# The expert loop's turns move from TensorE to VectorE in 32x32 squares, with a new order of the contraction and loops of four tiles

## The chip, the core and the metric

One core of one Trainium2 chip runs the kernel. The metric is the device time of one execution in microseconds (us), the median of several runs. Five engines work side by side, each with its own instruction stream: TensorE (PE, with its weight loads shown apart as PEld), VectorE (DVE), ScalarE (ACT), GpSimd (POOL) and SyncE (SP). SP issues most of the transfers and POOL issues the indirect ones. They wait for each other only through semaphores.

## The reference, cut to what matters

One layer of a hybrid backbone over 512 latent tokens of width 1024 (and 256 context tokens): a mixer (attention and a linear recurrence), then a mixture of experts. The change is almost all in the mixture:

```python
aff = sigmoid(h @ router_w)                    # h = rms(x) * norm_ffn * (1 + sc) + sh, (512, 1024)
# two experts for each token, out of 16, gates normalised
for e in range(16):
    y = (silu(h @ w1[e]) * (h @ w3[e])) @ w2[e]   # w1, w3: (1024, 512)   w2: (512, 1024)
    out = out + gates[:, e:e+1] * y
x = x + g_fx * out
```

All data are float32.

## The kernel before, in words

**Stages.** Up to about 387 us the kernel does the mixer, the residual and the router's products. VectorE then works out a plan: each expert's tokens are cut into tiles of 32 tokens, at least two tiles for each expert. This input gives 44 tiles, by expert in the order of the loop 3, 2, 2, 2, 4, 3, 2, 3, 5, 3, 2, 2, 4, 3, 2, 2. From about 412 us on the expert loop runs over these tiles; I number them 0 to 43. At the end SP copies the sums out.

**A tile.** A token's row of 1024 numbers lies in DRAM as four quarters of 256, and in SBUF a tile is 128 partitions (4 quarters x 32 tokens) x 256. For each tile:

- POOL gathers the 128 quarter rows from `xn_quarters` into one of two buffers `xg` (`gather`, L482), once the index column `cur_g` has been written by ACT (`gather_index`, L738) and the buffer has been emptied.
- ACT copies `xg` to `xrow` (`next_rows`, L731), which empties `xg`. PE turns it with two 128x128 transposes into PSUM (`turn_rows`, L1628), VectorE scales and shifts it by `ab2` (`rows_ready`, L1259) into `hsT`.
- PE multiplies by w1 and w3 (`products`, L1614: 32 matmuls, each recorded twice, so x64), ACT applies silu (`gate_half`, L723), VectorE multiplies the halves (`gated`, L1266).
- PE turns the result with one transpose (`turn_act`, L1634), ACT copies it to `eT` (`turned`, L727), PE multiplies by w2 (`rows_out`, L1638: 16 matmuls, x32).
- VectorE scales the rows by the gate into one of two buffers `ysb` (`scaled`, L1270) and POOL adds them to `out_quarters` in DRAM by an indirect transfer with addition (`scatter`, L486), with an index column `cur_s` that ACT wrote (`scatter_index`, L744).

On PE the order of a tile is `products(n)`, `turn_rows(n+1)`, `rows_out` for tile n-1, `turn_act(n)`. On POOL a scatter and a gather alternate: `fetch_rows` (L503), then `store_rows` (L509). Both indirect transfers go through POOL's queue, q0; the weights go through SP's, q1.

**Weights.** SP streams them in 48 chunks of 2 MB, three for each expert: chunk 3e and 3e+1 are the two halves of the contraction of w1 and w3, chunk 3e+2 is w2 (`fetch`, L309). There are 11 homes for them (`homes`, L245), so the first 11 chunks come early, and from chunk 11 on a chunk waits until the chunk 11 places before it has been used (L340 to L345). In DRAM a chunk is read as `(k p) n`: a run of consecutive bytes is one row, 2 KB for w1 and w3 and 4 KB for w2.

Of the kernel before, what the change touches and what calls it, by code (L numbers as in the profile page):

```python
# [56 lines left out]
def build(nc, x, c, ctx_in, c_ctx, w_mod, b_mod, norm_mix, norm_ffn, w_in, w_out, q_gain, k_gain, na_bias,  # L57
# [3 lines left out]
    xn_dram = nc.dram_tensor("xn_quarters", (TRASH + 2 * P, QD), F32, kind="Internal").ap()  # L61
    acc_dram = nc.dram_tensor("out_quarters", (TRASH + 2 * P, QD), F32, kind="Internal").ap()
# [6 lines left out]
    with ctx:  # L69
# [57 lines left out]
        row_sum = small[:, 32:34]  # L127
        hsum = sb("hsum", [P, 2, 2, H])
# [8 lines left out]
        xrow = hx[:, 4864:5120]  # L137
# [5 lines left out]
        ysb = [pre[:, 21632:21888], pre[:, 21888:22144]]  # L143
# [21 lines left out]
        cur_s = [nc.alloc_sbuf_tensor_at(f"cur_s{par}", [P, 1], I32, offset=hx_at + 4 * (4096 + 192 + 8 * par))  # L165
                 for par in range(2)]
# [15 lines left out]
            rank_m oh_ready oh_used rank_ps plan_in xn_out tok_ready t_ps sil_ready act_ready t2_ps  # L182
            t2_ev fin_out misc_in rw_in h_ps xm_ready hs_ready yt_ps y_ev cur_g_ready cur_s_ready
            acc_in gf_ps gf_ev lane_set sil_warm pad_ready xr_ready bank_z row_sum_ready scale_ready
            hc_ready h2_ev2""".split()
# [7 lines left out]
         xn_out, tok_ready, t_ps, sil_ready, act_ready, t2_ps, t2_ev, fin_out, misc_in, rw_in, h_ps,  # L193
         xm_ready, hs_ready, yt_ps, y_ev, cur_g_ready, cur_s_ready, acc_in, gf_ps, gf_ev, lane_set,
         sil_warm, pad_ready, xr_ready, bank_z, row_sum_ready, scale_ready, hc_ready, h2_ev2) = [sem(n) for n in names]
        xg_in = [sem(f"rows_in{par}") for par in range(2)]
        y_in = [sem(f"sums_in{par}") for par in range(2)]
# [56 lines left out]
        def chunk13(e, part):  # L254
            return homes[(3 * e + part) % NH].rearrange("p (k w n) -> p k w n", k=4, w=2)
# [4 lines left out]
        H_, X_, T_, Y_ = B[2], B[0], B[4], B[5]  # L260
# [21 lines left out]
        def _(sp):  # L282
# [49 lines left out]
            sp.wait_ge(xn_out1, 8 * NT + 16)  # L332
            sp.wait_ge(h2_ps, 2 * NT)
            fetch(8)
            sp.wait_ge(acc_in, 16 * NT + 32)
# [10 lines left out]
            half = sp.value_load(plan[0:1, 3 * NE - 1:3 * NE], min_val=NE - 2, max_val=MAXT // 2 - 2)  # L346
            added = sp.snap(16 * half + 32)
            for par in range(2):
                sp.wait_ge(y_in[par], added)
# [7 lines left out]
        def _(pool):  # L357
# [49 lines left out]
            g.dma_start(rw[:], router_w.rearrange("(k p) e -> p k e", p=P)).then_inc(rw_in, 16)  # L407
# [60 lines left out]
            for z in range(2):  # L468
                g.dma_start(xn_dram[TRASH + P * z:TRASH + P * (z + 1), :], xn[:, 0, 0:QD]).then_inc(
                    (xn_out, xn_out1)[z], 16)  # L470
# [4 lines left out]
            for z in range(2):  # L475
                g.dma_start(acc_dram[TRASH + P * z:TRASH + P * (z + 1), :], x2[:, 0, 0:QD]).then_inc(acc_in, 16)
            link(g.iota(pad_i[:], [[0, 32], [P, 2]], base=TRASH, channel_multiplier=1))
# [14 lines left out]
            pool.wait_ge(xn_out1, 8 * NT + 16)  # L492
            pool.wait_ge(acc_in, 16 * NT + 32)
# [3 lines left out]
            for n in (2, 3):  # L497
                pool.wait_ge(xr_ready, n - 1)
                gather(slot_tok[:, n:n + 1], n % 2)
            pool.wait_ge(plan_in, 1)  # L500
            half = pool.value_load(plan[0:1, 3 * NE - 1:3 * NE], min_val=NE - 2, max_val=MAXT // 2 - 2)

            def fetch_rows(h, par):  # L503
                indexed = pool.snap(2 * h + par - 3)
                pool.wait_ge(cur_g_ready, indexed)
                pool.sem_inc(pool_step, 1)
                gather(cur_g[par][:], par)

            def store_rows(h, par):  # L509
                indexed, scaled, stored = (pool.snap(n) for n in (2 * h + par + 1, 2 * h + par + 2, 16 * h))  # L510
# [3 lines left out]
                pool.wait_ge(y_in[par], stored)  # L514
                pool.sem_inc(pool_step, 1)
                scatter(par)

            for u in range(2):
                pool.wait_ge(cur_g_ready, u + 1)
                gather(cur_g[u][:], u)  # L520
                pool.wait_ge(cur_s_ready, u + 1)
                pool.wait_ge(y_ev, u + 2)
                scatter(u)
            with pool.Fori(1, half) as h:
                for par in range(2):
                    fetch_rows(h + 2, par)
                    store_rows(h, par)
            fetch_rows(half + 2, 0)
            for n in range(4):
                store_rows(half + n // 2, n % 2)  # L530

        @block.scalar
        def _(act):
# [193 lines left out]
            def turned(n):  # L727
                act.wait_ge(t2_ps, n + 1)
                a.activation(eT, T_[:, 0:P], ACT.Copy).then_inc(t2_ev, 1)  # L729

            def next_rows(h, par):  # L731

                act.wait_ge(xg_in[par], 16 * h + 16)
                if not isinstance(h, int) or h + par:
                    act.wait_ge(t_ps, 2 * h + par)
                a.activation(xrow, xg[par], ACT.Copy).then_inc(xr_ready, 1)  # L736

            def gather_index(h, par):  # L738

                act.wait_ge(xg_in[par], 16 * h)  # L740
                act.wait_ge(xr_ready, 2 * h + par - 1)
                a.activation(cur_g[par][:], slot_tok[:, bass.ds(2 * h + par, 1)], ACT.Copy).then_inc(cur_g_ready, 1)

            def scatter_index(h, par):  # L744

                if not isinstance(h, int) or h:
                    act.wait_ge(y_in[par], 16 * h)
                a.activation(cur_s[par][:], slot_tok[:, bass.ds(2 * h + par, 1)], ACT.Copy).then_inc(cur_s_ready, 1)  # L748
# [3 lines left out]
            next_rows(0, 0)  # L752
            act.wait_ge(plan_in, 1)
            half = act.value_load(plan[0:1, 3 * NE - 1:3 * NE], min_val=NE - 2, max_val=MAXT // 2 - 2)
            next_rows(0, 1)

            def activation(gt):
# [3 lines left out]
                if not isinstance(gt, int) or gt:  # L761
                    act.wait_ge(yt_ps, gt)
                turned(gt)

            activation(0)
            next_rows(1, 0)
            gather_index(2, 0)
            activation(1)
            next_rows(1, 1)
            gather_index(2, 1)  # L770
            scatter_index(0, 0)
            activation(2)
# [921 lines left out]
```

## Time and profile before

| what | us |
|---|---|
| median of 3 runs | 710.21 (709.7 to 711.41) |
| the profiled execution, whole | 711.65 |
| its span, first to last instruction | 709.9 |
| PE busy | 635.1 (89%) |
| DVE busy | 345.1 (49%) |
| ACT busy | 229.4 (32%) |
| POOL busy | 176.4 (25%) |

A busy share is an average over stages. The queries used below are: the chain of work that ended last, in order of time (start, us, what); the timeline of one engine or of a stretch (start, us, engine, line, operation, output<-input, and in brackets the idle time before it); groups of instructions by line; and the DMA view of a short stretch. PEclk is the TensorE clock that was granted, in tenths of full speed.

### The profile page before, as it was taken

To read this page: it belongs to the slowest core of one execution; us is meant where nothing else is said; L and a number is where in the kernel's file an instruction comes from. 1 tells how busy PE (TensorE), PEld (TensorE's weight loads), DVE (VectorE), ACT (ScalarE), POOL (GpSimd) and SP (SyncE) were. 2 spreads that over 40 slices of the span, in tenths; PEclk is the share of its full clock that TensorE was granted. 3 is DMA by queue.
4 is the path that set the end of the run, shared out by engine and by line. 5 is a ranking of instruction groups with operands and counts; after the bars stand their busy time and mean duration, and the time that the engine had idled before them with its cause. 6 is when DMAs were issued, how large, how long until landed. Compare 5 with 4: busy or idle time off the path is not lost.

```text
span 709.9 us, 15144 instructions
## 1 busy us (share of the span) xinstructions
PE 635.1 (89%) x5905; PEld 350.0 (49%) x5905; DVE 345.1 (49%) x823; ACT 229.4 (32%) x587; POOL 176.4 (25%) x201
## 2 busy tenths in 40 slices
PE   0799999899998999999999249999999999999991
PEld 0446544455444445555558225555555555555550
DVE  4513999556678957877755712222222222222220
ACT  5312201258887114555654001221112211222110
POOL 3033682000000001000003022344444444344431
PEclk9999999989999999999996559999999999999996
DMA  7999338711105359400059963999999999999924
GB/s 218 387 317 296 127 118 294 239 60 42 76 1 178 116 188 269 123 2 1 1 167 408 414 256 93 371 382 381 379 378 379 378 382 376 379 382 383 330 37 133
DMA packets 83507, 167.55 MB, mean 236 GB/s; under 512 B 4148, under 2 KB 26320, under 8 KB 83456
## 3 DMA queue, kind: packets, MB, share of 16 engines
q1 hardware_dynamic: 71856, 145.78, 56.6%
q0 software_dynamic: 11472, 21.00, 11.8%
q8 instruction: 38, 0.62, 0.4%
q14 instruction: 13, 0.11, 0.0%
q10 hardware_dynamic: 128, 0.04, 0.0%
HBM read 155.52 MB, written 12.60 MB: 237 GB/s over the span
## 4 chain that ended last, share of the span: by engine, by line
PE 67%; DVE 17%; DMA 5%; issue 5%; ACT 4%; SPq 1%; POOLq 0%; DVEq 0%; ACTq 0%
PE bank L1623 23%; PE bank L1646 12%; PE bank L1432 7%; PE bank L1540 6%; DMA ring<-in_w_mod_dram 4%; DVE acct L886 3%; PE bank L1357 3%; DVE gax L886 3%; PE bank L1631 2%; PE bank L1517 2%; PE bank L1492 2%; PE bank L1503 2%; DVE pre L904 2%; PE bank L1636 2%; PE bank L1321 1%
## 5 line engine op out<-in xcount | busy, mean ns | idle before, releaser
L1432 PE MATMUL bank<-ring,hx 128*128 128x512 f32 x256 | 114.9, 605 | 2.7 <-DVE mix L939 2.7
L487 POOL DMA_INDIRECT out_quarters<-pre,cur_s x44 | 69.6, 1582 | 146.3 <-ACT cur_s L748 124.2
L1268 DVE TENSOR_TENSOR pre<-pre,bank 128x128 f32<-128x128 f32 x44 | 12.7, 288 | 161.8 <-ACT pre L725 161.8
L1432 PEld LDWEIGHTS bank<-ring,hx 128*128 128x128 f32 x256 | 49.0, 194 | 60.2 <-issue 59.5
L1623 PE MATMUL bank<-pre 128*32 128x256 f32 x1248 | 75.1, 387 | 2.1 <-DVE pre L1264 1.4
L1623 PE MATMUL bank<-ring,pre 128*32 128x256 f32 x1152 | 68.5, 384 | 0.3
L1540 PE MATMUL bank<-ring,mix 128*128 128x512 f32 x128 | 60.7, 594 | 0.0
L1623 PEld LDWEIGHTS bank<-pre 128*32 128x32 f32 x1248 | 41.7, 111 | 26.8 <-issue 3.0
L725 ACT ACTIVATE pre<-bank 128x128 f32<-128x128 f32 x44 | 12.2, 278 | 118.4 <-PE bank L1623 118.4
L1623 PEld LDWEIGHTS bank<-ring,pre 128*32 128x32 f32 x1152 | 38.1, 111 | 23.1 <-issue 2.7
L1357 PE MATMUL bank<-hx,ring 128*128 128x256 f32 (+1 forms) x128 | 43.7, 502 | 1.4 <-DVE hx L864 1.4
L729 ACT ACTIVATE pre<-bank 128x128 f32<-128x128 f32 x44 | 12.2, 278 | 97.3 <-PE bank L1636 97.3
L1646 PE MATMUL bank<-pre 128*32 128x256 f32 x704 | 42.5, 382 | 0.6 <-DVE pre L1275 0.6
L1275 DVE SCALAR_TENSOR_TENSOR pre<-bank,hx,pre 128x256 f32<-128x256 f32 x44 | 21.3, 484 | 44.3 <-PE bank L1646 44.3
L456 POOL DMA_DIRECT2D pre<-pre x1 | 0.6, 561 | 153.6 <-ACT pre L661 153.6
L1357 PEld LDWEIGHTS bank<-hx,ring 128*128 128x128 f32 x128 | 24.7, 195 | 20.1 <-issue 17.4
L1646 PE MATMUL bank<-ring,pre 128*32 128x256 f32 x544 | 32.9, 382 | 0.0
L886 DVE SCALAR_TENSOR_TENSOR acct<-ring,cs,acct 128x256 f32<-128x256 f32 x56 | 29.4, 525 | 2.0
L466 POOL DMA_DIRECT2D xn_quarters<-pre x4 | 2.2, 544 | 110.5 <-DVE pre L1063 110.5
L1540 PEld LDWEIGHTS bank<-ring,mix 128*128 128x128 f32 x128 | 21.7, 190 | 14.7 <-issue 14.7
L1646 PEld LDWEIGHTS bank<-pre 128*32 128x32 f32 x704 | 20.8, 109 | 15.5 <-issue 3.5
L1631 PE MATMUL bank<-ident,hx 128*128 128x128 f32 x90 | 19.9, 304 | 8.9 <-ACT hx L736 8.9
(282 smaller groups left out, 1033.7 us busy)
## 6 DMA issues: line engine op xcount, KB each, us to landing
pre<-in_exp_w_dram SPq DMA_DIRECT2D x28, 1024.0 KB, 17.8
ring<-in_exp_w_dram SPq DMA_DIRECT2D x24, 1024.0 KB, 17.4
ring<-in_w_mod_dram SPq DMA_DIRECT2D x16, 1024.0 KB, 5.2
pre<-in_exp_w_dram SPq DMA_DIRECT2D x8, 2048.0 KB, 17.8
ring<-in_exp_w_dram SPq DMA_DIRECT2D x6, 2048.0 KB, 18.1
ring<-in_w_in_dram SPq DMA_DIRECT2D x5, 2048.0 KB, 16.5
ring<-in_w_mod_dram SPq DMA_DIRECT2D x4, 2048.0 KB, 19.5
mix<-in_exp_w_dram SPq DMA_DIRECT2D x6, 1024.0 KB, 19.4
```

What stands on the lines that cost most here:

```text
L487: g.indirect_dma_start(out=acc_dram, out_offset=bass.IndirectOffsetOnAxis(ap=cur_s[par][:].bitcast(U32), axis=0), in_=ysb[par], in_offset= ...
L886: ins = v.scalar_tensor_tensor(out=dst, in0=src[:, k, :], scalar=cs[:, k, 0:1], in1=dst, op0=ALU.mult, op1=ALU.add)
L904: ins = v.scalar_tensor_tensor(out=uc[:, m, 0:UO], in0=ur[:, k:k + UO], scalar=tap(k), in1=uc[:, m, 0:UO], op0=ALU.mult, op1=ALU.add)
L1275: v.scalar_tensor_tensor(out=ysb[par], in0=Y_[:, 0:QD], scalar=gate_tab[:, bass.ds(2 * h + par, 1)], in1=gfx4, op0=ALU.mult, op1=ALU.mult) ...
L1357: ins = te.matmul(B[bank][:, 0:n], slot[:, k, P * m:P * (m + 1)], hxT[:, k, lo:lo + n], start=(k == 0), stop=(k == KD - 1))
L1432: ins = te.matmul(B[bank][:, :], hxT[:, k, P * j:P * (j + 1)], slot[:, k, :], start=(k == 0), stop=(k == KD - 1))
L1492: ins = te.matmul(B[SB[p % 2][z]][:, c0:c0 + 256], qT[o:o + HD, m, P * t:P * (t + 1)], kT[o:o + HD, m, k0:k1], start=True, stop=True)
L1503: ins = te.transpose(B[5][:, P * q:P * (q + 1)], prob[:, b, P * q:P * (q + 1)], ident[:])
L1540: ins = te.matmul(B[YB[hf]][:, :], mix[:, k, P * j:P * (j + 1)], out_at[hf][0][:, k, :], start=(k == MW), stop=(k == MW - 1))
L1623: ins = te.matmul(H_[R * q:R * (q + 1), 0:2 * P].rearrange("p (w n) -> p w n", w=2), hsT[:, at:at + R], w[:, k % 4, :, P * q:P * (q + 1)], ...
L1631: ins = te.transpose(X_[:, P * z:P * (z + 1)], xrow[:, P * z:P * (z + 1)], ident[:])
L1646: ins = te.matmul(Y_[R * q:R * (q + 1), 0:QD], eT[:, R * c:R * (c + 1)], w[:, c, QD * q:QD * (q + 1)], start=(c == 0), stop=(c == 3))
```

## The change

It has five parts.

1. **Turns.** PE's three transposes of a tile go, with ACT's two copies around them. VectorE turns `xg` straight into `xm` and `eact` into `eT` with a transpose of 32x32 squares. A square can't mix partitions of different groups of 32, so the numbers of a row are taken with a stride of 8 (of 4 for `eact`) instead of in runs of 128.
2. **Order of the contraction.** To match, everything that is contracted with these rows is read as `(p k) n` instead of `(k p) n`: w1, w3, w2, `router_w`, and the shift, scale and gain vectors (three new small transfers `ffn_row`). A run in DRAM is now 4 rows: 8 KB for w1 and w3, 16 KB for w2. The SBUF layout of a w1/w3 chunk changes from (k w n) to (w k n), so the run is consecutive there too. PE's transposes of the router read `xn` with a stride of 8, and `reduce_mod` has 8 matmuls instead of 4.
3. **Buffers.** Four buffers `ysb` and four index columns `cur_s` instead of two. `xg` and `cur_g` stay at two.
4. **Loops** on ACT, DVE and POOL take four tiles in a turn instead of two, and the number of tiles is rounded up to a multiple of four (44 stays 44).
5. **Padding rows**: 4 x 128 spare rows in `xn_quarters` and `out_quarters` instead of 2 x 128, written by one transfer instead of two.

The weights:

```diff
-                        sp.dma_start(chunk13(e, part)[:, :, w, :], src[0, ORDER[e], 512 * part:512 * (part + 1), :].rearrange(
-                            "(k p) n -> p k n", p=P)).then_inc(csem[n % NH], 16)
+                        sp.dma_start(chunk13(e, part)[:, :, w, :],
+                                     src[0, ORDER[e]].rearrange("(p k) n -> p k n", p=P)[
+                                         :, 4 * part:4 * part + 4, :]).then_inc(csem[n % NH], 16)
...
-                    sp.dma_start(chunk2(e), exp_w2[0, ORDER[e]].rearrange("(k p) n -> p k n", p=P)).then_inc(csem[n % NH], 16)
+                    sp.dma_start(chunk2(e), exp_w2[0, ORDER[e]].rearrange("(p k) n -> p k n", p=P)).then_inc(
+                        csem[n % NH], 16)
```

On POOL, the loop after (`fetch_rows(h + 1, i)` gathers tile 4h+i+4, `store_rows(h, i)` adds tile 4h+i):

```diff
+            for i in range(4):
+                pool.wait_ge(cur_g_ready, i + 1)
+                gather(cur_g[i % 2][:], i % 2)
+                pool.wait_ge(cur_s_ready, i + 1)
+                pool.wait_ge(y_ev, i + 2)
+                scatter(i)
+            with pool.Fori(1, last) as h:
+                for i in range(4):
+                    fetch_rows(h + 1, i)
+                    store_rows(h, i)
+            for i in range(4):
+                store_rows(last, i)
```

On ACT (`activation(n)` is the silu of tile n, `index_ahead(h, i)` the `gather_index` of tile 4h+i+5):

```diff
+            def gather_index(h, i):
+                act.wait_ge(xg_in[i % 2], 32 * h + 16 * (i // 2))
+                act.wait_ge(rows_taken, 4 * h + i - 1)
+                a.activation(cur_g[i % 2][:], slot_tok[:, bass.ds(4 * h + i, 1)], ACT.Copy).then_inc(cur_g_ready, 1)
...
+            with act.Fori(1, last) as h:
+                for i in range(4):
+                    activation(4 * h + i + 1)    
+                    index_ahead(h, i)
+                    scatter_index(h, i)
```

On DVE (`take_ahead(h, i)` is `take_rows` of tile 4h+i+3):

```diff
+            def take_rows(h, i):
+                n = 4 * h + i
+                dve.wait_ge(xg_in[i % 2], 32 * h + 16 * (i // 2) + 16)
+                if not isinstance(n, int) or n:
+                    dve.wait_ge(hs_ready, n)
+                v.transpose(blocks(xm), xg[i % 2].rearrange("p (t b) -> p b t", b=KD)).then_inc(rows_taken, 1)
+                dve.wait_ge(rows_taken, n + 1)
+                v.tensor_tensor(blocks(xm), blocks(xm), wide(0), ALU.mult).then_inc(xm_scaled, 1)
+
+            def shift_rows(n):
+                if not isinstance(n, int) or n:
+                    dve.wait_ge(h_ps, n)
+                dve.wait_ge(xm_scaled, n + 1)
+                v.tensor_tensor(blocks(hsT), blocks(xm), wide(1), ALU.add).then_inc(hs_ready, 1)
+
             def gated(n):
                 dve.wait_ge(sil_ready, n + 1)
+                if not isinstance(n, int) or n:
+                    dve.wait_ge(t2_ev, n)
                 v.tensor_tensor(eact, esil, H_[:, P:2 * P], ALU.mult).then_inc(act_ready, 1)
+                if not isinstance(n, int) or n:
+                    dve.wait_ge(yt_ps, n)
+                dve.wait_ge(act_ready, n + 1)
+                v.transpose(eT.rearrange("p (b t) -> p b t", b=4), eact.rearrange("p (t b) -> p b t", b=4)).then_inc(t2_ev, 1)
...
+            with dve.Fori(1, last) as h:
+                for i in range(4):
+                    tile_step(4 * h + i + 1)
+                    scaled(h, i)
+                    take_ahead(h, i)
```

On PE:

```diff
-                turn_rows(base + 1)
                 if e:
                     rows_out(base, e - 1)
-                turn_act(base)
                 with pe.Fori(1, tiles) as t:
                     gt = base + t
                     products(gt, e, False)
-                    turn_rows(gt + 1)
                     rows_out(gt, e)
-                    turn_act(gt)
```

## Rows read from the trace of the kernel before

**Rows 1.** The page's 40 slices of the span (17.7 us each).

```profile
PEclk9999999989999999999996559999999999999996
DMA  7999338711105359400059963999999999999924
```

**Rows 2.** The chain that ended last, window 500:520: start us, us, what.

```profile
502.14 3.66 PE bank L1623 x64
505.80 0.37 PE bank L1631 x2
506.17 1.86 PE bank L1646 x32
508.04 0.26 PE bank L1636
```

**Rows 3.** Groups by line and shape, window 430:710: busy us, mean ns, idle before.

```profile
L1275 DVE SCALAR_TENSOR_TENSOR pre<-bank,hx,pre 128x256 f32<-128x256 f32 x44 | 21.3, 484 | 44.3 <-PE bank L1646 44.3
...
L1264 DVE TENSOR_TENSOR pre<-pre,ab 128x256 f32<-128x256 f32 x43 | 18.3, 425 | 1.5
...
L1268 DVE TENSOR_TENSOR pre<-pre,bank 128x128 f32<-128x128 f32 x43 | 12.4, 288 | 155.2 <-ACT pre L725 155.2
```

**Rows 4.** The chain that ended last, window 390:450, where the loop begins.

```profile
418.51 0.42 ACT hx L736
418.98 0.70 PE bank L1631 x2
...
427.87 0.43 DVE pre L1264
428.35 3.66 PE bank L1623 x64
```

**Rows 5.** Timeline, window 500:515: from emptying a gather buffer to the next gather.

```profile
508.58 0.42 ACT L736 ACTIVATE hx<-hx 128x256 f32<-128x256 f32 x1
...
510.47 1.58 POOL L487 DMA_INDIRECT out_quarters<-pre,cur_s  x1 [3.52 <-ACT cur_s L748]
...
512.36 1.00 POOL L483 DMA_INDIRECT hx<-xn_quarters,cur_g  x1 [0.31 <-issue]
```

**Rows 6.** L483, issue to landing, windows 450:550, 561:563, 591:593, 671:700, in this order.

```profile
DMA to landing us min/median/max: 5.6/6.3/7.1
...
DMA to landing us min/median/max: 5.6/5.6/5.6
...
DMA to landing us min/median/max: 7.0/7.0/7.0
...
DMA to landing us min/median/max: 2.7/3.5/4.2
```

**Rows 7.** DMA view, windows 564.5:567.5 and 594:598: packets, MB, share of 16 engines.

```profile
q1 hardware_dynamic: 392, 0.78, 70.9%
...
q1 hardware_dynamic: 439, 1.21, 78.5%
```

**Rows 8.** DMA view, windows 375:379, 403:406 and 475:500.

```profile
DMA packets 750, 1.61 MB, mean 401 GB/s; under 512 B 31, under 2 KB 31, under 8 KB 750
...
DMA packets 320, 1.25 MB, mean 416 GB/s; under 512 B 2, under 2 KB 2, under 8 KB 319
...
q1 hardware_dynamic: 3437, 8.45, 87.4%
q0 software_dynamic: 770, 1.05, 18.3%
```

**Rows 9.** Timeline of SP, issues of the w2 chunks 11, 23 and 47.

```profile
438.15 0.37 SPq L316 DMA_DIRECT2D pre<-in_exp_w_dram  x1
...
504.81 2.59 SPq L316 DMA_DIRECT2D ring<-in_exp_w_dram  x1
...
657.36 2.05 SPq L316 DMA_DIRECT2D pre<-in_exp_w_dram  x1
```

**Rows 10.** The page's DMA issues: KB each, median us to landing.

```profile
pre<-in_exp_w_dram SPq DMA_DIRECT2D x8, 2048.0 KB, 17.8
```

**Rows 11.** Timeline, window 664:710: products of tile 42 and of tile 43.

```profile
680.13 3.66 PE L1623 MATMUL bank<-ring,pre 128*32 128x256 f32 x64
...
686.21 3.66 PE L1623 MATMUL bank<-ring,pre 128*32 128x256 f32 x64
```

More of the change, by code:

```diff
@@ L164, in build @@
                  for par in range(2)]
[L165 to L166 removed]
+        cur_s = [nc.alloc_sbuf_tensor_at(f"cur_s{par}", [P, 1], I32, offset=hx_at + 4 * (5376 + 8 * par))
+                 for par in range(4)]
         lane4 = sb("lane4", [P, 1])
@@ L345, in _ @@
                 fetch(n)
-            half = sp.value_load(plan[0:1, 3 * NE - 1:3 * NE], min_val=NE - 2, max_val=MAXT // 2 - 2)
-            added = sp.snap(16 * half + 32)
-            for par in range(2):
+            last = sp.value_load(plan[0:1, 3 * NE - 1:3 * NE], min_val=NE // 2 - 1, max_val=MAXT // 4 - 1)
+            added = sp.snap(16 * last + 16)
+            for par in range(4):
                 sp.wait_ge(y_in[par], added)
@@ L511, in store_rows @@
                 pool.wait_ge(cur_s_ready, indexed)
                 pool.wait_ge(y_ev, scaled)
-                pool.wait_ge(y_in[par], stored)
+                pool.wait_ge(y_in[i], stored)
                 pool.sem_inc(pool_step, 1)
[L516 to L530, printed above, removed]
+                scatter(i)
+            for i in range(4):
+                pool.wait_ge(cur_g_ready, i + 1)
+                gather(cur_g[i % 2][:], i % 2)
+                pool.wait_ge(cur_s_ready, i + 1)
+                pool.wait_ge(y_ev, i + 2)
+                scatter(i)
@@ L1290, in _ @@
-            gated(0)
-            rows_ready(1)
-            tile_step(1)
-            scaled(0, 0)
-            tile_step(2)
-            scaled(0, 1)
-            with dve.Fori(1, half + 1) as h:
-                tile_step(2 * h + 1)
-                scaled(h, 0)
-                tile_step(2 * h + 2)
-                scaled(h, 1)
-            tile_step(2 * half + 3)
-            scaled(half + 1, 0)
-            scaled(half + 1, 1)
+            last = dve.value_load(plan[0:1, 3 * NE - 1:3 * NE], min_val=NE // 2 - 1, max_val=MAXT // 4 - 1)
@@ new lines, in tile_step, with take_ahead @@
+            def tile_step(n):
+                shift_rows(n + 1)
+                gated(n)
+            def take_ahead(h, i):
+                if i < 1:
+                    take_rows(h, i + 3)
+                else:
+                    take_rows(h + 1, i - 1)
+            tile_step(0)
+            take_rows(0, 2)
+            for i in range(4):
+                tile_step(i + 1)
+                scaled(0, i)
+                take_ahead(0, i)
+            with dve.Fori(1, last) as h:
+                for i in range(4):
+                    tile_step(4 * h + i + 1)
+                    scaled(h, i)
+                    take_ahead(h, i)
@@ L1305, in _ @@
+            for i in range(2):
+                tile_step(4 * last + i + 1)
+                scaled(last, i)
+                if i < 1:
+                    take_ahead(last, i)
+            gated(4 * last + 3)
+            scaled(last, 2)
+            scaled(last, 3)
         @block.tensor
```

206 lines of the change are left out of this document (80 added, 126 removed).

## The prediction, on record before the changed kernel was timed

> **What bounds the kernel now.** I read the page's slices first, then the chain in the expert loop, then the DMA view. From slice 25 on PE's clock is at full speed and the DMA engines are as busy as they get [rows 1]: two resources look full, so the question is which one sets the pace and how far behind the other is. The chain answers for a tile: products 3.66 us, turn_rows 0.37, rows_out 1.86, turn_act 0.26, all PE (the next products stand at 3.59, a usual period is 6.09) [rows 2]. PE waits for no weight there. The weights are fed ahead through 11 homes: SP issues w2 of expert 3 (chunk 11) at 438.15, chunk 23 at 504.81 and chunk 47 at 657.36 [rows 9]. The last 24 chunks took 152.6 us, 6.36 us each, and 17.8 us from issue to landing [rows 10] means that about three chunks are queued all the time. So the stream runs at its own speed and PE at its own. An expert of 2.75 tiles costs the stream 3 x 6.36 = 19.1 us and PE 2.75 x 6.09 = 16.7 us; the stream is the slower one and lives on its head start. Chunk 47 lands at about 657.4 + 17.8 = 675, chunk 46 at about 668.8; PE wants chunk 46 in the middle of the products of tile 42, at 680.13 + 1.8 = 682 [rows 11]. What is left of the head start is 13 us.
>
> **The turns.** PE loses 0.37 + 0.26 = 0.63 us in each of 43 tiles: 27.1 us [rows 2]. At the loop's start ACT's copy (0.42) and two PE transposes at the lower clock (0.70) give way to one VectorE transpose, 0.43 by the nearest row: 0.7 us [rows 3, 4]. Products of tile 1 stood behind turn_act and two VectorE operations until 428.35; now they stand behind one addition and `gated`, about 0.6 us less [rows 4]. Sum of PE's own path: 28.4 us.
>
> VectorE's new transposes aren't in the trace. Nearest rows: 425 ns for 128x256 and 288 ns for 128x128 [rows 3]. Lower bound, those less nothing; upper bound, twice them, if the stride of 8 halves the rate. I take 0.43 and 0.29. After rows_out ends VectorE has to do: transpose of `eact` 0.29, `scaled` 0.48, transpose 0.43, scaling 0.43, together 1.6 us, inside 3.6 us of products. Twice the transposes makes 2.35, still inside. After products end it has the shift 0.43 and `gated` 0.29, together with waits 0.9 us, inside rows_out's 1.86. So VectorE's work costs nothing, and if that cover were gone it would cost its own length in each tile. ACT loses a copy of each kind; it waits most of the time.
>
> **The weight stream.** A run grows from 2 to 8 KB and from 4 to 16 KB. No row shows such a run. With 2 KB packets alone the engines moved 401 GB/s, with 4 KB packets alone 416 [rows 8]. Lower bound: no gain. Upper bound: time per byte as a constant plus a cost for each packet gives 424 at 8 KB and 428 at 16 KB, which is 4.5% less time for the weights as a whole. Of the 229 us of chunks 11 to 46, q0 has 18.3 / 105.7 = 17%, so 190 us are weights and 8.6 us could go [rows 8]. I take the upper end, since 401 to 416 is a slope and not a limit. The stream also starts 2.1 us earlier (home 0 is free after products of tile 2).
>
> The Trainium skill (DMA: Bandwidth & Descriptors, Bandwidth, Where 436 GB/s comes from) says that HBM limits one core to about 358 GB/s whatever the packet. The 401 to 416 GB/s of rows 8 are above that, so the trace disagrees; by that rule the stream would gain nothing from long runs, which is the third rival.
>
> **The gathers.** This is where I expect most of the gain to go. `xg` keeps two buffers, so gather m+2 hangs on gather m: landing, VectorE's transpose (0.43), ACT's two index copies, POOL's scatter (1.58) that stands before the gather in program order, the gather's issue. From the end of ACT's copy of `xg` (508.58 + 0.42 = 509.00) to the next gather's issue (512.36) it is 3.36 us [rows 5]; with the transpose it is 3.8. With L for issue to landing, two tiles can't take less than L + 3.8. Before, 6.3 + 3.8 = 10.1 us [rows 6] lay inside 2 x 6.09 = 12.2. After, 2 x 5.46 = 10.9 us is PE's own pace, so L may grow from 6.3 to 7.1 only.
>
> L depends on the other queue. Without the stream it is 2.7; in the stream it was 5.6 with packets of 2 KB (0.78 MB in 392) and 7.0 with packets of 2.75 KB on average (1.21 MB in 439) [rows 6, 7]. A gather's engine has 8 scatter packets and 2 gather packets of 1 to 4 KB before the landing (128 and 32 packets over 16 engines); if each of them lets one weight packet pass, ten weight packets count. In rows 7 a packet of 2.0 KB takes 3 us x 16 x 70.9% / 392 = 87 ns and one of 2.75 KB 4 us x 16 x 78.5% / 439 = 114 ns, so 73 ns for 2 KB more. Then ten packets of 8 KB add 2.2 us to 5.6, ten of 16 KB 5.1: L is 7.8 and 10.7. Lower bound: L stays 6.3. Upper bound: the slope of L itself between 5.6 and 7.0 (1.4 us for 0.75 KB) is far steeper than ten packets explain and has no end at 16 KB; I cut it at 1.5 us above my value. I take 7.8 and 10.7, the value with a mechanism behind it.
>
> The period of a tile is then (7.8 + 3.8) / 2 = 5.8 us in the two thirds of the time with 8 KB packets and 7.25 in the third with 16 KB: on average 1 / (0.667 / 5.8 + 0.333 / 7.25) = 6.2 us (an L of 8.6), as long as the stream lasts. That is 0.1 more than before. Afterwards PE's 5.46 holds.
>
> The Trainium skill says the same of the mechanism (DMA: Bandwidth & Descriptors, Queues, rings and completion order): each engine serves its queues in turn and drains a packet before it switches. It speaks against this change, since long runs make long packets. The rows agree as far as 4 KB; none shows 8 or 16.
>
> **The sum.** Products of tile 2 start at 432.5 and of tile 3 at 437.9. Gather 6 is issued 4.7 us after the latter (0.9 for VectorE's transpose and `scaled`, 0.43, 3.36), at about 442.7, and lands at 450.7; products of a tile start 1.8 us after its gather's landing (transpose, scaling, shift, `gated`, waits), those of tile 6 at 452.5 and of tile m at 452.5 + 6.2 (m - 6). The stream ends at 675 - 2.1 - 8.6 = 664, when the loop stands at tile 40.1. The rest goes at 5.46: tile 43 starts at 664 + 2.9 x 5.46 = 680, against 686.2 before [rows 11]. That is 6.2 us, and 0.4 us at the end for the turn that no longer stands before the last rows_out: span 709.9 - 6.6 = 703.3. The profiled execution took 711.65 in all, 1.4 more than the median, so I forecast the median of the runs as 710.2 - 6.6, about 703.5 us.
>
> **What I cost at nothing.** The scatter's longer landing: four `ysb` and `cur_s` let it take four tiles. A scatter shares the queue with the gathers and will land about as late; with two buffers its landing would have stood in `scaled`'s way from some 9 us on. The three small transfers and one more padding write (256 KB each, 0.6 us of DMA time) lie in stretches where POOL waits. `reduce_mod` and the strided router transposes: 0 to 2 us, I take 0. The larger gather L at the very first tile: 0 to 1.5 us, I take 0, in the range.
>
> **The rivals.**
> 1. *The gathers don't slow down* (L stays under 7.1). For it: the median of 6.3 moved little over many mixtures. Against it: 5.6 against 7.0. Then PE's path is 28.4 us shorter and wants chunk 46 at 654; it lands at 668.8 - 2.1 - 8.6 = 658. Gain 28.4 - 4 = 24.4: 686 us.
> 2. *The gathers slow down more than by ten packets*: one mechanism, POOL's queue, on the other side of no change. Each us of L costs 0.5 us of the period, and a tile not done while the stream lasts costs 5.46 afterwards: 211 / 6.2 / 6.2 x 0.5 x 5.46 = 15 us in all. The whole is slower than before from an average L of 9.0 on; it gives 714 us at 9.3 and 725 at 10. For it: the steep step from 5.6 to 7.0. Against it: at 6.3 in the median no mixture went over 7.1 [rows 6].
> 3. *The stream gains nothing from long runs* and the gathers stay quick: chunk 46 at 666.7, PE waits 12.6 us, gain 15.8: 694 us.
> 4. *Turns cost VectorE far more*: the two transposes would need 4 times the nearest rows to fill the 3.6 us of products; under 2 in 100.
>
> **How the numbers follow.** The forecast case (694 to 708 us) has 0.42, rival 1 (684 to 692) 0.23, rival 2 (708 to 725) 0.30, rival 3 0.04, the rest 0.01. The range 684 to 717 leaves the worse half of rival 2 out, and a bit below. The likeliest case's own range is 694 to 708. A difference under 0.3% (2.1 us) can't be told from none: faster than 708.1 are the forecast, rivals 1 and 3 less an edge: 0.67; between 708.1 and 712.3 a third of rival 2 and that edge: 0.12; slower 0.21.
>
> **What would show it.** Right: L483 lands after 8 to 10 us in the stream; L1623 on PE idles before the products and is released by VectorE, which waits for a gather; the period is near 6.2 until some 664 and 5.46 after; weight packets of 8 and 16 KB. Rival 1: PE without idle time at 5.46, and waits for the last chunks. Rival 3: PE waits for DMA from tile 33 on. Wrong altogether if VectorE's transposes take over 2 us, if packets stay at 4 KB or below, or if PE's clock falls in its new pauses.

## The result and the profile after

The changed kernel takes **720.53 us** (median of 4, 719.8 to 720.68) beside 710.81 us for the kernel before (median of 4, 709.7 to 711.44): ratio 1.0149, 95% interval 1.0114 to 1.0184. It is slower; the forecast was 703.5 us, range 684 to 717. A second set of runs on another chip gave 718.75 (716.72 to 722.03), ratio 1.0131 (1.0111 to 1.0151). The profiled execution has a span of 718.8 us; the forecast was 703.3, so 15.5 us of span have to be accounted for.

The page's slices of the changed kernel (18.0 us each), beside [rows 1]; the third line is GB/s:

```profile
PEclk9989999999999999999996559999999999999996
DMA  8999338611205349400049965999999969999524
GB/s 217 387 307 298 120 118 307 218 60 37 79 1 176 118 175 272 122 2 1 1 174 424 396 264 178 394 395 404 395 394 404 393 217 400 399 403 391 133 38 132
```

In the loop the DMA engines move 391 to 404 GB/s, more than the 371 to 383 of the page before, but for one slice at 217. PE is no longer busy all the time, as the windows show (us, then busy time and count of PE, PEld, DVE, ACT, POOL, then granted clock, DMA share, GB/s):

```profile
475.00:500.00 25.00, 19.71 (x335) 12.12 (x328) 8.87 (x22) 1.73 (x9) 8.59 (x7) 0.93 1.04 398
500.00:525.00 25.00, 20.51 (x344) 13.79 (x340) 8.58 (x20) 1.95 (x11) 9.71 (x9) 0.93 1.03 400
...
575.00:600.00 25.00, 24.57 (x416) 17.00 (x412) 9.77 (x24) 2.32 (x12) 12.15 (x10) 0.94 0.78 271
```

What the loop waits for stands in the waits of the window 430:710 (us in total, times, longest):

```profile
DVE pre L1245 <- DMA hx<-xn_quarters,cur_g: 50.7, 17, 7.2
DVE pre L1245 <- DMA pre<-xn_quarters,cur_g: 47.1, 16, 6.8
...
PE bank L1634 <- DVE pre L1261: 31.7, 18, 4.5
```

L1245 is VectorE's transpose of a gathered tile. It waits for 33 of the 44 gathers, 98 us in all, and PE's products wait behind it. The chain of the changed kernel has no PE in it in this stretch (start, us, what); compare [rows 2], which is PE alone:

```profile
492.53 10.69 DMA hx<-xn_quarters,cur_g
503.24 0.66 DVE pre L1245
...
504.19 0.21 ACT cur_s L739
...
505.31 1.58 POOL out_quarters L490
...
507.19 10.53 DMA hx<-xn_quarters,cur_g
...
521.75 7.62 DMA hx<-xn_quarters,cur_g
...
533.34 9.00 DMA hx<-xn_quarters,cur_g
...
546.38 10.57 DMA hx<-xn_quarters,cur_g
```

Each ring of it is one buffer's two tiles: gather, transpose, two index copies, scatter, next gather. Four rings take 546.38 - 492.53 = 53.85 us, so 13.46 us for two tiles and 6.73 for one. Their gathers take 9.5 us on average, the rest of a ring 4.0. For the whole stretch the products of tiles 7, 37 and 43 in PE's timeline give the period:

```profile
463.55 1.93 PE L1634 MATMUL bank<-hx,pre 128*32 128x256 f32 x32 [0.23 <-issue]
...
663.75 1.93 PE L1634 MATMUL bank<-ring,pre 128*32 128x256 f32 x32 [1.24 <-DVE pre L1261]
...
695.79 3.66 PE L1634 MATMUL bank<-ring,pre 128*32 128x256 f32 x64
```

Tiles 7 to 37 take 200.2 / 30 = 6.67 us each while the stream runs (forecast 6.2), and the last six 32.04 / 6 = 5.34 (forecast 5.46 behind the stream). Tile 43 starts at 695.79; it started at 686.21 before [rows 11], and the forecast was 680.

VectorE's transposes, by line and shape (busy us, mean ns | idle before):

```profile
L1265 DVE STREAM_TRANSPOSE pre<-pre 128x128 f32<-128x128 f32 x44 | 18.4, 419 | 28.6 <-PE bank L1647 25.0 <-issue 1.1 <-DVE pre L1261 0.6
...
L1245 DVE STREAM_TRANSPOSE pre<-hx 128x256 f32<-128x256 f32 x21 | 13.6, 647 | 50.7 <-DMA hx<-xn_quarters,cur_g 50.7
```

The weights came in longer packets. DMA view, window 475:500, beside the last two lines of [rows 8]:

```profile
q1 hardware_dynamic: 962, 9.02, 87.0%
q0 software_dynamic: 677, 0.89, 16.3%
```

9.4 KB a packet instead of 2.5, and 9.02 MB instead of 8.45: the stream did gain, 7%. A weight packet holds its engine for 25 x 16 x 87.0% / 962 = 362 ns.

Ahead of the loop something else was lost. `reduce_mod` has 8 matmuls instead of 4 (each recorded twice). Its four calls in the kernel before and in the changed one, from PE's timelines:

```profile
113.09 0.95 PE L1390 MATMUL bank<-ones,acct 128*128 128x1 f32 x8
127.78 0.95 PE L1390 MATMUL bank<-ones,acct 128*128 128x1 f32 x8
142.73 1.87 PE L1390 MATMUL bank<-ones,acct 128*128 128x1 f32 x8 [4.01 <-DVE acct L886]
249.35 0.95 PE L1390 MATMUL bank<-ones,acct 128*128 128x1 f32 x8
```

```profile
114.06 2.08 PE L1398 MATMUL bank<-ones,acct 128*64 128x1 f32 x16
131.70 2.08 PE L1398 MATMUL bank<-ones,acct 128*64 128x1 f32 x16
145.49 2.08 PE L1398 MATMUL bank<-ones,acct 128*64 128x1 f32 x16
251.79 2.08 PE L1398 MATMUL bank<-ones,acct 128*64 128x1 f32 x16
```

That is 8.3 us instead of 4.7. From 100 to 150 us PE is busy for all of the 50 us; before, it was busy for 45.99, and the missing 4.01 are the pause in front of the third call. The calls are also followed by slower products. These are the mixer's products behind the fourth call, the same 32 records before and after:

```profile
250.16 13.98 PE L1432 MATMUL bank<-ring,hx 128*128 128x512 f32 x32
```

```profile
253.80 15.70 PE L1442 MATMUL bank<-ring,hx 128*128 128x512 f32 x32
```

The granted clock from 254 to 265 us was 1.00 before and 0.85 after. Behind all four calls these products take 14.00, 7.11, 9.53 and 13.98 us before, and 15.70, 8.83, 8.83 and 15.70 after. They end at 264.14 and at 269.50, 5.4 us apart. The slot table, the plan's last operation, was made at 410.70 us before and at 416.06 after, again 5.4 us apart: nothing is lost between these products and the slot table. So 5.4 us of the 15.5 were gone before the loop began, and 10.1 went in the loop.

### The profile page after: what moved, and what is told of

The parts are those of the page before. It is cut to its first block, busy times and chain, and to the rows that moved or that the text cites. A ratio compares the mean times of both kernels' runs of the same rounds, so it can differ in the third digit from the quotient of the medians.

```text
span 718.8 us, 14786 instructions
## 1 busy us (share of the span) xinstructions
PE 616.0 (86%) x5803; PEld 368.8 (51%) x5803; DVE 386.2 (54%) x909; ACT 200.3 (28%) x498; POOL 176.4 (25%) x201
## 4 chain that ended last, share of the span: by engine, by line
PE 49%; DMA 23%; DVE 10%; issue 7%; ACT 4%; POOL 3%; SPq 1%; POOLq 0%; ACTq 0%; DVEq 0%
DMA hx<-xn_quarters,cur_g 20%; PE bank L1442 11%; PE bank L1634 6%; PE bank L1550 6%; PE bank L1365 6%; PE bank L1372 4%; POOL out_quarters L490 3%; PE bank L1647 3%; DMA ring<-in_w_mod_dram 2%; PE bank L1527 2%; PE bank L1502 2%; PE bank L1513 2%; DVE pre L1245 2%; PE bank L1329 1%; PE bank L1398 1%
## 5 line engine op out<-in xcount | busy, mean ns | idle before, releaser
L1634 PEld LDWEIGHTS bank<-pre 128*32 128x32 f32 x1248 | 49.3, 116 | 56.2 <-DVE pre L1254 34.6
L733 ACT ACTIVATE cur_g<-slot_tok 128x1 int32 (+1 forms) x41 | 8.3, 203 | 204.6 <-DVE pre L1245 204.6
L1634 PEld LDWEIGHTS bank<-ring,pre 128*32 128x32 f32 x1152 | 44.4, 113 | 34.8 <-DVE pre L1254 13.5
L490 POOL DMA_INDIRECT out_quarters<-pre,cur_s x22 | 34.9, 1585 | 81.5 <-ACT cur_s L739 61.9
L490 POOL DMA_INDIRECT out_quarters<-hx,cur_s x22 | 35.1, 1595 | 71.2 <-ACT cur_s L739 56.7
L1245 DVE STREAM_TRANSPOSE pre<-pre 128x256 f32<-128x256 f32 x22 | 14.2, 645 | 53.8 <-DMA pre<-xn_quarters,cur_g 47.1
L1245 DVE STREAM_TRANSPOSE pre<-hx 128x256 f32<-128x256 f32 x22 | 14.2, 647 | 50.8 <-DMA hx<-xn_quarters,cur_g 50.7
L1254 DVE TENSOR_TENSOR pre<-pre,ab 128x256 f32<-128x256 f32 x44 | 18.7, 425 | 39.0 <-PE bank L1634 37.0
L1265 DVE STREAM_TRANSPOSE pre<-pre 128x128 f32<-128x128 f32 x44 | 18.4, 419 | 28.6 <-PE bank L1647 25.0
L1647 PEld LDWEIGHTS bank<-pre 128*32 128x32 f32 x704 | 27.4, 110 | 12.3 <-DVE pre L1265 1.4
L727 ACT ACTIVATE pre<-bank 128x128 f32<-128x128 f32 x44 | 12.1, 276 | 72.4 <-PE bank L1634 71.3
```

Of the source, the lines that this page charges most:

```text
L490: g.indirect_dma_start(out=acc_dram, out_offset=bass.IndirectOffsetOnAxis(ap=cur_s[par][:].bitcast(U32), axis=0), in_=ysb[par], in_offset= ...
L1245: v.transpose(blocks(xm), xg[i % 2].rearrange("p (t b) -> p b t", b=KD)).then_inc(rows_taken, 1)
L1254: v.tensor_tensor(blocks(hsT), blocks(xm), wide(1), ALU.add).then_inc(hs_ready, 1)
L1265: v.transpose(eT.rearrange("p (b t) -> p b t", b=4), eact.rearrange("p (t b) -> p b t", b=4)).then_inc(t2_ev, 1)
L1634: ins = te.matmul(H_[R * q:R * (q + 1), 0:2 * P].rearrange("p (w n) -> p w n", w=2), hsT[:, R * k:R * (k + 1)], w[:, k % 4, :, P * q:P * ( ...
L1647: ins = te.matmul(Y_[R * q:R * (q + 1), 0:QD], eT[:, R * c:R * (c + 1)], w[:, c, QD * q:QD * (q + 1)], start=(c == 0), stop=(c == 3))
```

## The experiments

Times are medians; the ratio is to the kernel before on the same chip, with its 95% interval. "Changed" is the kernel after the change.

**1. Only the long runs.** The kernel before, with one part of the change:

```diff
-            return homes[(3 * e + part) % NH].rearrange("p (k w n) -> p k w n", k=4, w=2)
+            return homes[(3 * e + part) % NH].rearrange("p (w k n) -> p k w n", k=4, w=2)
...
-                        sp.dma_start(chunk13(e, part)[:, :, w, :], src[0, ORDER[e], 512 * part:512 * (part + 1), :].rearrange(
-                            "(k p) n -> p k n", p=P)).then_inc(csem[n % NH], 16)
+                        sp.dma_start(chunk13(e, part)[:, :, w, :],
+                                     src[0, ORDER[e]].rearrange("(p k) n -> p k n", p=P)[
+                                         :, 4 * part:4 * part + 4, :]).then_inc(csem[n % NH], 16)
...
```

> The kernel before, with the weights alone read in runs of 8 and 16 KB (the products then pair weights with the wrong inputs; nothing else changes). Theory A (POOL's queue waits behind long weight packets, and the gather chain sets the pace): a gather lands after 10 to 11 us instead of 6.3, two tiles take L + 3.8 = 14.3 us, the period in the stream is 7.0 to 7.2 instead of 6.09, and the whole is 15 to 25 us slower than before, near 730. Theory B (the new order of VectorE, or its slow transposes, sets the pace in the changed kernel): period 6.09 as before, gathers may land late but nobody waits, 705 to 711.

Measured: 722.5 us (721.13 to 726.63), ratio 1.0193 (1.0147 to 1.0238): slower by some 12 us, less than the 15 to 25 expected. Tiles 7 to 37 take 6.55 us each, less than the expected 7.0 to 7.2 and more than the 6.1 before. The profiled execution had its slot table at 405.25 us, 5.4 earlier than the one before, so from there to the end it is 15 us longer. L485 is its gather; its landing in the window 450:640, beside the first line of [rows 6], and its waits:

```profile
DMA to landing us min/median/max: 2.8/9.6/11.4
```

```profile
DVE pre L1277 <- DMA out_quarters<-pre,cur_s: 64.1, 27, 4.3
...
ACT hx L738 <- DMA hx<-xn_quarters,cur_g: 39.6, 16, 5.2
```

The long runs alone take the gather's landing from 6.3 to 9.6 us, and with two result buffers `scaled` waits for scatters as well.

**2. All but the long runs.** The changed kernel with the weights read as before (the edit of experiment 1 the other way round).

> The changed kernel, with the weights alone read as before in runs of 2 and 4 KB (again wrong pairs in the products). Theory A: a gather lands after 6 to 7 us, PE has no pause between tiles, the period is 5.46, PE then waits for the last weight chunks, and the whole comes to about 700 (28 us of turns won, 5 lost ahead of the loop, 12 lost to the stream). Theory B: it stays within 3 us of the changed kernel, 717 to 722.

Measured: 700.41 us (699.35 to 701.96), ratio 0.9866 (0.9827 to 0.9906). VectorE hardly waits for gathers; PE waits for weights instead (window 430:680):

```profile
PE bank L1632 <- DMA ring<-in_exp_w_dram: 8.4, 3, 3.9
...
PE bank L1632 <- DMA pre<-in_exp_w_dram: 7.9, 3, 3.4
```

PE's waits for weights are 16.3 us in all. So of the change's two halves one gains 10.5 us and the other loses 11.6, each against the kernel before; the long runs cost 20 us in the changed kernel.

**3. Four gather buffers.** The changed kernel with the long runs kept; four `xg` and `cur_g`, gathers issued two tiles sooner:

```diff
-        xg = [pre[:, 20480:20736], hx[:, 4608:4864]]
+        xg = [pre[:, 20480:20736], hx[:, 4608:4864], hx[:, 5440:5696], hx[:, 5696:5952]]
...
-                    fetch_rows(h + 1, i)
+                    fetch_rows(h, i)
...
-                act.wait_ge(rows_taken, 4 * h + i - 1)
+                act.wait_ge(rows_taken, 4 * h + i - 3)
```

> The changed kernel with four gather buffers and index columns instead of two, and each gather issued six tiles ahead instead of four. Long weight runs stay. Theory A: a gather still lands after 10 us or more, but nobody waits for it; period 5.46, clock at full speed in the loop, 690 to 695. Theory B: no change, 717 to 722. If PE's pauses come from something else on VectorE, the period stays over 6.

Measured: 693.16 us (690.33 to 693.88), ratio 0.9752 (0.9711 to 0.9794). The landing is as long as ever (9.6 us in the median, a little less than the 10 expected), and nobody waits for it. L486 in the window 450:640, and the chain:

```profile
DMA to landing us min/median/max: 8.5/9.6/11.4
```

```profile
503.19 3.45 PE bank L1634 x64
506.64 1.73 PE bank L1647 x32
508.77 3.66 PE bank L1634 x64
512.43 1.73 PE bank L1647 x32
```

This is what shows the cause in the loop: same run length, same landing, 27 us less, because a slow landing is no longer in a ring of one buffer's two tiles. Tiles 7 to 32 take 5.33 us each. What holds PE up now is the weight stream, and the clock falls behind its waits (PE's timeline):

```profile
601.92 3.21 PE L1634 MATMUL bank<-pre 128*32 128x256 f32 x32 [2.61 <-DMA pre<-in_exp_w_dram]
...
608.15 2.62 PE L1634 MATMUL bank<-pre 128*32 128x256 f32 x32 [3.02 <-DMA pre<-in_exp_w_dram]
...
662.13 3.64 PE L1634 MATMUL bank<-ring,pre 128*32 128x256 f32 x32 [4.05 <-DMA ring<-in_exp_w_dram]
```

Such a group takes 1.94 us elsewhere; the granted clock was 0.86 in the windows 600:625 and 650:675.

**4. Half of the small matmuls.** `range(KD // 2)` for `range(KD)` in `reduce_mod`.

> The changed kernel with 4 instead of 8 matmuls in each of the four calls of reduce_mod (half of the sums for the FFN's shift and scale are left out; their routing may differ). If the 5.3 us that the changed kernel loses ahead of the expert loop come from these matmuls on PE, the loop starts 4 us earlier and the whole is 716 to 717. If they come from something else there, the start stays within 1 us. A different routing would show as another number of tiles.

Measured: 736.85 us (730.93 to 739.01), ratio 1.036 (1.0318 to 1.0402). A miss as an experiment: half of the shift and scale sums are missing, the tokens go to other experts, and that makes 48 tiles instead of 44 (L1254 runs x48). Only the front can be read: the slot table was made at 411.55 us, 4.5 earlier than in the changed kernel. Single executions turned out to differ by about as much (experiments 9 to 12), so alone it shows little.

**5 and 6. Which run length.** The changed kernel with only w2 read in 4 KB runs, and with only w1 and w3 in 2 KB runs.

> The changed kernel with w2 alone read in runs of 4 KB (w1 and w3 stay at 8 KB; rows_out then pairs weights with the wrong inputs). Theory A, a packet of weights passes for each packet of POOL's queue: a gather lands after 8 to 9 us, two tiles take 12 to 13 us, between the changed kernel and the one with short runs only: 703 to 712. If the length of the packet doesn't count and only runs over 4 KB as such do, it stays at 717 to 721.

> The changed kernel with w1 and w3 read in runs of 2 KB and w2 alone in 16 KB (the products pair weights with the wrong inputs). Theory A: the gathers are quick (6 to 7 us) for two thirds of the stream and slow (11 us and more) for one third: 702 to 712.

Measured: 701.28 us (697.48 to 703.46), ratio 0.9883 (0.9816 to 0.9951), and 699.62 (697.05 to 701.92), ratio 0.9882 (0.9817 to 0.9946). Both are below what was expected (703 to 712 and 702 to 712). Waits of the kernel with 8 KB runs alone:

```profile
DVE pre L1244 <- DMA hx<-xn_quarters,cur_g: 57.4, 18, 4.6
...
DVE pre L1244 <- DMA pre<-xn_quarters,cur_g: 47.8, 19, 3.8
```

VectorE still waits 105 us for gathers, as long as in the changed kernel (98), and yet the time is 19 us shorter. A wait of VectorE costs only what is longer than its slack: the longest ones fell from 7.2 to 4.6 us, and PE's products waited 19.2 us for VectorE's work instead of 31.7. The landings in its chain from 496 to 543 are 6.3, 8.2, 8.9, 7.2 and 7.8, on average 7.7, which makes a ring of 7.7 + 4.0 = 11.7 us, 5.8 for a tile. Taking either long run away brings 19 or 21 us back, as much as taking both away (20), though w2 is one third of the weights and w1 and w3 are two. A ring that costs nothing until it is longer than PE's own two tiles (10.9 us in the forecast) would do that; the length at which the loss begins was not measured by itself.

**7. Two result buffers.** Experiment 3, where `scaled` waits for the scatter two tiles back instead of four:

```diff
-                if not isinstance(h, int) or h:
-                    dve.wait_ge(y_in[i], 16 * h)
+                if i >= 2:
+                    dve.wait_ge(y_in[i - 2], 16 * h + 16)
+                elif not isinstance(h, int) or h:
+                    dve.wait_ge(y_in[i + 2], 16 * h)
```

> The kernel with four gather buffers, where scaled of tile n also waits until the scatter of tile n-2 has landed, as it would with two result buffers. The scatter lands after 10 to 12 us here and two tiles of PE take 10.9: VectorE then waits for scatters, the period is 6.3 to 6.7, and the whole comes to 712 to 722 against 693. If the four result buffers are worth nothing, it stays at 691 to 695.

Measured: 708.87 us (706.57 to 713.5), ratio 1.0002 (0.9971 to 1.0034), beside 0.9752 with four: the four result buffers are worth about 2.5%, some 18 us, once scatters are slow too. It is a little less than expected (712 to 722 us), and a size that the prediction had named and not priced. Waits of VectorE:

```profile
DVE pre L1274 <- DMA out_quarters<-hx,cur_s: 53.3, 18, 4.5
...
DVE hx L1274 <- DMA out_quarters<-pre,cur_s: 45.6, 17, 5.5
```

**8. The best version.** Experiment 3, `reduce_mod` with its four matmuls of before, and shift and scale brought into the new order by two pairs of small transfers through DRAM:

```diff
-                for k in range(KD):
-                    ins = te.matmul(B[7][HD * (n % 2):HD * (n % 2 + 1), k:k + 1],
-                                    acct[:, :].rearrange("p (m k) -> p m k", k=KD)[:, :, k], ones[:, 0:1], start=True,
-                                    stop=True)
+                for q in range(4):
+                    ins = te.matmul(B[7][:, q:q + 1], acct[:, P * q:P * (q + 1)], ones[:, 0:1], start=True, stop=True)
...
+            for z in range(2):
+                g.dma_start(perm_dram[z].rearrange("(k p) -> p k", p=P), ab_k[:, z, :],
+                            allow_slow_non_contiguous=True).then_inc(perm_out, 16)
+            pool.wait_ge(perm_out, 32)
+            for z in range(2):
+                g.dma_start(ab2[:, z, :], perm_dram[z].rearrange("(p k) -> p k", p=P)).then_inc(ab_in, 16)
```

> The kernel with four gather buffers, where reduce_mod has its 4 matmuls back and the FFN's shift and scale are put into the new order by two pairs of small transfers through DRAM, which lie in front of the router. If those matmuls are the whole loss ahead of the expert loop, the loop starts 4 to 5 us earlier: 687 to 690 against 693. If the transfers delay the router's rows, less.

Measured: 688.55 us (686.71 to 690.94), ratio 0.9722 (0.9673 to 0.977). It beats both kernels. Against experiment 3 the intervals overlap, and the slot table was made at 411.36 us, 1.4 earlier than there and not 4 to 5: the time came as expected, its reason not.

**9 to 12. What the small matmuls cost.** The slot table's time differed by 3 us and more between profiles of kernels with the same front, so the 5.4 us (5.3 in the expectations) needed pairs on one chip: the changed kernel again, the same with the edit of experiment 8 alone, experiment 3 again, and experiment 8 again.

> The changed kernel itself, for the variation of its front and of its time beside the other three of this set. In six profiled kernels with eight small matmuls in a reduce_mod call the slot table (the plan's last operation) was ready at 412.3 to 416.5 us, in four kernels with four of them at 405.3 to 411.6, so part of the 5.3 us between the two first profiles may be the spread of single executions. Theory A (the eight matmuls cost about 4 to 5 us): slot table at 415 to 417, time 719 to 722. Theory B (they cost 1 to 2 us and the rest was spread): slot table near 413, time 717 to 720.

> The changed kernel with reduce_mod's four matmuls of before, the shift and scale of the experts brought into the new order by two pairs of small transfers through DRAM, while the mixer's products run; nothing is left out. The gathers keep their two buffers. Theory A: slot table ready 4 to 5 us earlier than in the changed kernel beside it, and as the chain of gathers follows the start of the loop, the time is 4 to 5 us shorter, 715 to 717. Theory B: 1 to 2 us shorter, 718 to 719. Third: the small transfers are late, ACT and VectorE wait for them before the router's rows, and nothing is won.

> The changed kernel with four gather buffers, as once before (693.2 us), here beside the same kernel with reduce_mod's four matmuls on the same chip. 691 to 694 us; slot table at 412 to 414 us.

> Four gather buffers and reduce_mod's four matmuls, as once before (688.6 us, on another chip). Theory A: 4 to 5 us below the kernel with four gather buffers and eight matmuls. Theory B: 1 to 2 us below it. Slot table at 410 to 412 us.

| kernel | us (6 runs) | ratio (95%) | slot table made |
|---|---|---|---|
| changed | 718.75 | 1.0131 (1.0111 to 1.0151) | 412.31 |
| changed, four matmuls | 715.72 | 1.0073 (1.0049 to 1.0098) | 407.16 |
| four gather buffers | 693.0 | 0.9768 (0.9741 to 0.9794) | 409.94 |
| four gather buffers, four matmuls | 689.47 | 0.9715 (0.969 to 0.9739) | 409.61 |

The medians differ by 3.0 and by 3.5 us, and in neither pair do the intervals touch, in the second by a hair. So the small matmuls cost about 3 to 4 us of the whole, a little under theory A and over theory B.

How they cost it is seen less well. In the 14 profiles the slot table was made between 409.94 and 416.45 us in the 8 kernels with eight matmuls (median 412.9), and between 405.25 and 411.55 in the 6 with four (median 410.2; the kernel before and experiment 4 are among them). The 32 records of products behind the fourth call take 15.70 us in seven of the eight, as in the changed kernel, and 13.98 to 14.00 in the eighth and in all six. So the slower clock goes with the eight matmuls and costs 1.7 us there. It also makes part of the spread, since it is missing behind the first call in most of the eight. But an earlier slot table isn't passed on one to one. In the first pair it came 5.2 us earlier, and tile 43 started 1.1 us earlier. In the four kernels with four gather buffers tile 34 starts at 612.5 to 613.5 us wherever the slot table stood between 409.61 and 412.73, since PE waits for weights there. By which way the second pair's 3.5 us come was not traced.

## Why the prediction was wrong

**What held.** The two bounds before (PE's own path and the weight stream) and the mechanism that took the gain: gathers of two buffers, slowed by the longer packets of the other queue, set the pace as long as the stream runs, and PE's own pace holds afterwards. Of the signs that it named, PE's idle time in front of the products, VectorE's wait for gathers and the long packets are in the profile; the period near 6.2 is not. Its sums for the cases without the ring come near. Experiment 2 is rival 3's case (no gain of the stream, quick gathers): 694, measured 700.4. Experiment 3 is rival 1's (the gathers hold nobody up): 686, measured 693.2. With 3 to 4 us for the small matmuls added, some 3 are left in both. That is partly luck, because larger terms stand against each other. PE waits longer for weights (16.3 us instead of 12.6, and 9.6 instead of 4), and in experiment 3 the clock of 0.86 in two windows of 25 us is worth 3.5 us in each. PE's tiles are quicker than forecast (5.33 instead of 5.46). The Trainium skill's limit of about 358 GB/s for one core (DMA: Bandwidth & Descriptors, Bandwidth), by which long runs gain nothing, is by a note of the same section the share of a core when both cores of a pair stream. With one core running it did not bind here: the slices show 391 to 404 GB/s.

**The first step that failed** is the size of L, the time from a gather's issue to its landing. "I take 7.8 and 10.7", on average 8.6, with the upper bound cut "at 1.5 us above my value". The rings show 9.5, so the case was rival 2's, which was put at 0.30. By the prediction's own rule, "15 us in all" for each us of L, 0.9 us more are 13.5 us, which gives 717, the upper end of the range. Measured: tile 7 starts 4.9 us later than forecast (463.55 instead of 458.7). Thirty tiles at 6.67 instead of 6.2 add 14.1 us. The last six take 32.0 us instead of the forecast's 35.3, which gives 3.3 back. So tile 43 is 15.8 us late, of which 10.9 came in the loop from tile 7 on; the rule is somewhat too steep.

The weight packets were sized rightly: the prediction's lengths, 306 ns for 8 KB and 598 for 16 KB, make 364 ns for the mixture, and 362 were measured, against 87 to 114 before. 5.6 + 10 x (0.362 - 0.087) = 8.35 us is what ten of them explain; the landing is over 1 us longer. The count of ten is short, too. The DMA view of a gather alone (kernel before, window 425:436) has 48 packets, 16 of them under 512 B, and a gather with its scatter has 192. That is 12 to an engine and not 10. An estimate with twelve is 5.6 + 12 x 0.275 = 8.9 us, if the small ones let a weight packet pass as well, which no run shows. The Trainium skill's rule of engines that serve their queues in turn, packet by packet (DMA: Bandwidth & Descriptors, Queues, rings and completion order), gives the direction, and the runs agree; it gives no count of packets for a landing. What the rest consists of stays open. The row that spoke for it stood in the prediction, the steep step from 5.6 to 7.0, and it was set aside for having no mechanism. It rested on two single gathers, but a slope that a model doesn't explain is still evidence against the model.

**The ring's fixed part** was 4.0 us instead of 3.8. The difference is the transpose: 0.65 us instead of the 0.43 taken, inside the bounds of one and two times the nearest row. The transpose of `eact`, 0.42 instead of 0.29, is hidden, as forecast.

**"`reduce_mod` and the strided router transposes: 0 to 2 us, I take 0"** was the second step that failed. Of the two, the strided transposes cost nothing in the two profiles: the 5.4 us are complete at 269.50 us, ahead of them, and grow no further. `reduce_mod` costs 3 to 4 us (experiments 9 to 12). Its cost was counted by the amount of arithmetic, but eight matmuls of half the width take 2.08 us and four of the full width 0.95. Nor was the clock counted. In the two first profiles the calls are 3.6 us longer, the products behind them 4.4 us longer, and the pause of 4.01 us in front of the third call is gone, which takes 4.0 off. The first call also starts 1.0 us later. Together this is 5.0 of the 5.4 us. That the eight matmuls are the reason of the clock's fall is shown only by its going with them in seven of eight profiles and in none of six without them.

**The sum.** 10.1 us in the loop and 5.4 ahead of it make the 15.5 us. Of the 5.4, 3 to 4 are what the small matmuls cost in the medians, and the rest is the spread of single executions. L alone would have put the time at the edge of the range; both terms together put it outside.

**PE's clock** fell in its pauses, which the prediction had named as a way to be wrong. PE's timeline shows a slower tile behind a pause of 2.10 us, and the next one as before:

```profile
539.70 5.35 PE L1634 MATMUL bank<-pre 128*32 128x256 f32 x64 [2.10 <-DVE pre L1261]
...
546.56 3.66 PE L1634 MATMUL bank<-pre 128*32 128x256 f32 x64
```

The granted clock of the window 525:550 is 0.93: 7% of 25 us, or 3.5 us at the lower of the two levels (1.2 instead of 2.4 GHz), costs the 1.7 us by which this tile is longer. The fall is real, and the chain of this stretch holds no PE at all, so the 1.7 us lie beside a gather and cost nothing. At 573.95 us it is different: there the slow tile stands in the chain itself, with the next two behind it, until 592 us:

```profile
573.95 5.35 PE bank L1634 x64
```

So the fall is a mark of the ring in most places and a cause of 1.7 us in one; what it costs in the whole loop was not tried by itself.

**The dip to 217 GB/s** is another mark. SP waited for a free home for 25 us (issues at 564.29 and 590.66), since the loop used up its experts late and the stream was quicker; while the stream stood still PE was busy 24.57 of 25 us. The slow gathers brake the stream, and the stream's pause lets the gathers catch up.

## What to carry to other kernels

Before a bulk transfer gets longer runs, look at who shares the DMA engines with it: here a small gather that someone waited for landed 3 us later behind the longer packets. Work out the ring of its buffer (landing, emptying, index, issue) against the pace of as many tiles as there are buffers. By the rings of this case, one within that pace costs nothing and a longer one costs its excess in each turn, and another pair of buffers is the cheap cure. Long runs and the deeper gathers belong together: the runs alone lost 12 us. With four gather buffers the kernel with long runs takes 693.2 us, and with two buffers and short runs it takes 700.4. Four buffers with short runs were not run, but with short runs VectorE hardly waits for a gather, so the 7 us are probably the runs'. Small matmuls in a full stretch are counted by number and not by columns, and so is what follows them: look at the granted clock of the products behind them.

## What the runs showed of the hardware

- VectorE's transpose in 32x32 squares of 128x256 float32, read with a stride of 8, takes 0.65 us; an addition of that size takes 0.43. The one of 128x128 with a stride of 4 takes 0.42, the product of that size 0.28. Which share the stride has was not separated.
- A gather of 128 KB lands in 6.3 us (median) beside a stream with runs of 2 and 4 KB, and in 9.6 beside one with 8 and 16 KB.
- A matmul with one column takes 0.12 us a record with 128 columns of weights (8 in 0.95 us) and 0.13 with 64 (16 in 2.08 us).
- Behind the eight small matmuls of a call the same 32 records of products (512 columns) took 15.70 us at a granted clock of 0.85, instead of 13.98 at 1.00.
